# Moving the turned activation to the front of SBUF, and the down projection's stationary operand behind the branch sum

## The reference, cut to what matters

```python
def swiglu(x, w_in, w_out):
    gate, up = jnp.split(x @ w_in, 2, axis=-1)
    return (jax.nn.silu(gate) * up) @ w_out
...
    for layer in range(DEPTH):
        ff = swiglu(rmsnorm(h, g[0]), ffn_w_in[layer, 0], ffn_w_out[layer, 0])
        h = h + 0.5 * rmsnorm(ff, g[1])
        ...                                   # mixer: attention, gated linear attention or RWKV
        ff = swiglu(rmsnorm(h, g[4]), ffn_w_in[layer, 1], ffn_w_out[layer, 1])
        h = h + 0.5 * rmsnorm(ff, g[5])
```

## Time and profile before

| What | us |
|---|---|
| median of 3 runs | 3006.59 (3006.22 to 3006.69) |
| the profiled execution | 3007.35 |
| its span, first to last instruction | 3005.4 |
| PE busy | 2882.7 |
| DVE busy | 2102.8 |
| ACT busy | 1448.9 |
| GB/s from and to HBM, mean over the span | 156 |

### The profile page before, as it was taken

The page is one execution under the profiler, slowest core; times in us unless marked ns, Lnnn a source line. Parts: engine busy times, 40 slices in busy tenths (PEclk is TensorE's granted clock), DMA queues, the critical chain, the costliest instruction groups (busy, mean ns, idle before and its releaser), DMA issues.

```text
span 3005.4 us, 44680 instructions
## 1 busy us (share of the span) xinstructions
PE 2882.7 (96%) x17202; PEld 2491.9 (83%) x17202; DVE 2102.8 (70%) x3035; ACT 1448.9 (48%) x1865; POOL 84.4 (3%) x94
## 2 busy tenths in 40 slices
PE   8998999999999999999999999998999999989998
PEld 7887787888888888888988878876887889978887
DVE  6767677776767777767767777766777775565676
ACT  5445545445544444563444454455445444444443
POOL 0000000000000000100120000000000000000000
PEclk9999999999999999999999999999999999999999
DMA  8643564663456566431016656643656656533662
GB/s 241 207 115 127 173 196 142 210 191 114 133 179 196 157 189 207 121 121 50 1 53 186 196 153 198 185 126 120 189 182 175 189 159 183 183 116 129 200 195 84
DMA packets 614848, 471.24 MB, mean 157 GB/s; under 512 B 40545, under 2 KB 572385, under 8 KB 614708
## 3 DMA queue, kind: packets, MB, share of 16 engines
q1 hardware_dynamic: 614564, 469.31, 51.7%
q10 hardware_dynamic: 144, 0.00, 0.0%
HBM read 466.37 MB, written 1.84 MB: 156 GB/s over the span
## 4 chain that ended last, share of the span: by engine, by line
PE 84%; DVE 8%; ACT 5%; issue 2%; DMA 0%; SPq 0%; PEldq 0%; ACTq 0%; DVEq 0%; PEld 0%
PE pair_bank L413 26%; PE pair_bank L414 14%; PE pair_bank L589 11%; PE out_banks L433 7%; PE out_banks L435 7%; PE out_banks L434 7%; PE out_banks L589 2%; DVE low L337 2%; ACT high L333 2%; PE pair_bank L406 1%; PE pair_bank L2200 1%; PE pair_bank L2188 1%; DVE h L733 1%; PE pair_bank L2184 1%; DVE y L723 1%
## 5 line engine op out<-in xcount | busy, mean ns | idle before, releaser
L337 DVE TENSOR_TENSOR low<-raw,high 128x3072 fp32r<-128x3072 f32 (+2 forms) x328 | 934.7, 2850 | 603.7 <-ACT high L333 602.9
L413 PE MATMUL pair_bank<-x_parts,high 128*128 128x512 f32 x3360 | 1179.1, 393 | 4.4 <-issue 2.4
L414 PE MATMUL pair_bank<-x_parts,low 128*128 128x256 f32 x3520 | 961.9, 280 | 0.0
L333 ACT ACTIVATE high<-raw 128x3072 fp32r<-128x3072 f32 (+2 forms) x328 | 774.0, 2360 | 255.2 <-PE out_banks L435 154.0
L413 PEld LDWEIGHTS pair_bank<-x_parts,high 128*128 128x128 f32 x3360 | 629.6, 187 | 150.3 <-issue 7.8
L414 PEld LDWEIGHTS pair_bank<-x_parts,low 128*128 128x128 f32 x3520 | 655.1, 189 | 10.7 <-DVE low L337 1.1
L463 ACT ACTIVATE sq_scratch<-pair_bank 128x512 f32<-128x512 f32 x220 | 131.6, 598 | 559.1 <-PE pair_bank L414 559.1
L433 PE MATMUL out_banks<-high,hid_h 128*128 128x512 f32 x880 | 348.5, 396 | 9.5 <-DVE hid_l L505 9.5
L434 PE MATMUL out_banks<-low,hid_h 128*128 128x512 f32 x880 | 347.9, 395 | 0.0
L435 PE MATMUL out_banks<-high,hid_l 128*128 128x512 f32 x880 | 347.8, 395 | 0.0
L589 PE MATMUL pair_bank<-high,x_parts 128*128 128x256 f32 x1216 | 232.1, 289 | 4.6 <-DVE x_parts L786 1.6
(11 more groups left out here) (374 smaller groups left out, 3060.6 us busy)
## 6 DMA issues: line engine op xcount, KB each, us to landing
raw<-in_ffn_w_in_dram SPq DMA_DIRECT2D x352, 512.0 KB
raw<-in_ffn_w_out_dram SPq DMA_DIRECT2D x176, 512.0 KB
raw<-in_ffn_w_dram SPq DMA_DIRECT2D x132, 512.0 KB
raw<-in_w_in_dram SPq DMA_DIRECT2D x32, 1024.0 KB
raw<-in_gla_w_in_dram SPq DMA_DIRECT2D x12, 1024.0 KB
raw<-in_rwkv_w_rkv_dram SPq DMA_DIRECT2D x12, 1024.0 KB
raw<-in_swa_w_qkv_dram SPq DMA_DIRECT2D x10, 1024.0 KB
raw<-in_swa_w_o_dram SPq DMA_DIRECT2D x8, 1024.0 KB
```

The lines of the kernel that those rows point to most:

```text
L333: nc.scalar.activation(high[u % SPLIT][:, lo:w], raw[u % RAW][:, lo:w], ACT.Copy).then_inc(high_ready, count)
L337: nc.vector.tensor_tensor(low[u % SPLIT][:, lo:w], raw[u % RAW][:, lo:w], high[u % SPLIT][:, lo:w].bitcast(F32), ALU.subtract).then_inc(we ...
L413: nc.tensor.matmul(o, H[:, w], x_parts[:, k, :], start=(k == 0), stop=False)
L414: last = nc.tensor.matmul(o[:, 0:SEQ], L[:, w], xh[:, k, :], start=False, stop=(k == KB - 1))
```

## The change

The allocation of `x_parts` is moved in front of the `raw` slots, and that of the four `hid` buffers from behind `hidden` to behind `y`. Nothing else is changed. Each engine's instructions are the same in the same order; only the addresses in them differ.

```diff
+        x_parts = sb("x_parts", [P, KB, 2 * SEQ], F32R)
         raw = [sb(f"raw{i}", [P, SLOT]) for i in range(RAW)]
         high = [sb(f"high{i}", [P, SLOT], F32R) for i in range(SPLIT)]
         low = [sb(f"low{i}", [P, SLOT], F32R) for i in range(SPLIT)]
         h = sb("h", [P, NT, D])
         y = sb("y", [P, NT, D])
-        x_parts = sb("x_parts", [P, KB, 2 * SEQ], F32R)
         xh, xl = x_parts[:, :, 0:SEQ], x_parts[:, :, SEQ:2 * SEQ]
+        hid_h = [sb(f"hid_h{i}", [P, SEQ], F32R) for i in range(2)]
+        hid_l = [sb(f"hid_l{i}", [P, SEQ], F32R) for i in range(2)]
         gain = [sb(f"gain{i}", [P, D]) for i in range(2)]
         gain_columns = [sb(f"gain_columns{i}", [P, KB]) for i in range(2)]
         silu = sb("silu", [P, SEQ])
         hidden = sb("hidden", [P, SEQ])
-        hid_h = [sb(f"hid_h{i}", [P, SEQ], F32R) for i in range(2)]
-        hid_l = [sb(f"hid_l{i}", [P, SEQ], F32R) for i in range(2)]
```

## The result

| | before | after |
|---|---|---|
| median, us | 3006.05 (3002.12 to 3007.37, 20 runs) | 3011.36 (3008.58 to 3016.67, 20 runs) |
| profiled execution: time / span, us | 3007.35 / 3005.4 | 3010.25 / 3008.3 |
| one unit, us | 8.35 | 8.39 |
| one down projection, us | 2.80 | 2.75 |
| gate and up: one pair, ns | 346.7 | 353.3 |

The changed kernel is slower: the ratio is 1.0022, with a 95% interval of 1.0016 to 1.0028. The forecast was 2989 us; the result lies 2 us beyond the upper end of the range, and on the other side of the time before.

A forecast was written before the change was run, and what follows sets the result against it. The prediction took PE's stream of matmuls, 96% busy, as the bound: 3006.6 - 17.6 (`hid` buffers) + 0 (`x_parts` and the rest) = 2989.0 us. Its own range was 2986 to 2992 us (0.58), the wide one 2986 to 3009 (0.85).

The forecast's parts named there:

- What bounds the kernel: Whole kernel: a stream of matmuls on PE, 96% busy, so time is their number times their pitch.
- The cause of the down projection's slow pitch: Down projection: 6.7 ns extra per matmul, laid to the `hid` buffers' place, 64 bytes beyond a multiple of 128, or high.
- The term for it: Down projection, L433 to L435: the `hid` buffers' move saves 6.7 ns on each of 2640 matmuls, 17.6 us.
- half of it: Down projection: some six of 12 matmuls stay at 232 ns, 9 us won, 2997.6 us; chance 0.06.
- The pairs: Gate and up, L413 and L414: the pairs stay at 346.7 ns, no change in time.
- The prediction's own sign for this: Profile after, gate and up: pairs at other than 346.7 ns would mean the move of `x_parts` counts.
- The term for `x_parts`: Matmuls reading `x_parts`, 10,288 counted: the move to a low address gives nothing, bounds 69 us either way.
- The waits: L433's wait for `hid_l`, 9.5 us in all, grows by less than 1 us; up to 0.8 us given back.
- The readings: Pitches from trace starts: 37 output-projection matmuls at 226.7 ns; after stalls, 6 at 232 and ten down-projection ones at 233.
- The one that named a time near the result, 3011.5 us: Low `x_parts` costs 6.7 ns a matmul: 3058 us if all pay, 3011.5 if only L413 does; chance 0.10.

The follow-up runs named there:

- The best kernel here: Kernel before with all 512-column matmuls ahead of the 256s, `hid` moved behind `y` on a multiple of 128, `x_parts` 64 bytes off: 2976.57 us, ratio 0.9895.

## Why the prediction was wrong, point by point

- **What bounds the kernel: right.** No wait of the changed kernel has grown by more than 2.3 us, and all that moved is pitch.
- **The cause of the down projection's slow pitch: right.** It is the alignment of the stationary operand and not its height, as the two kernels with `gain_columns` moved show. The Trainium skill, "SBUF — State Buffer", section "Who interferes with whom", has PE wait on nobody. Whatever makes the step, these runs show that a matmul's pitch does depend on where its operand starts, 226.7 or 233.3 ns.
- **The term for it: mis-sized.** The prediction gave all 12 matmuls of a down projection the settled pitch, 2640 x 6.7 = 17.6 us. Measured are 10.9 us within the down projections. The first five stay slow, at 232 ns in the mean, even with no stall ahead. This was the rival "half of it", with its 9 us, to which I gave 0.06. The earlier trace rows had shown the slow start, and I had tied it to stalls.
- **The pairs: the step that failed.** "It can act only through a pitch that depends on where an operand lies", and the pairs' operands keep their alignment, so they were given 346.7 ns again. They went to 353.3: +14.6 us, more than the down projection gives. The pitch of alternating lengths is not a property of their operands alone. At the addresses of these two kernels it has two values, and moving `hid`, which the pairs don't read, moved 189 units from the one to the other. So the alignment of `hid` acts on the pairs through the down projection ahead of them. The prediction's own sign for this was wrong too: it said that pairs at other than 346.7 ns would convict the move of `x_parts`.
- **The term for `x_parts`: right.** Its count of 10,288 left out, among others, the 160 matmuls of L406 and the 192 of the output projection, which would have widened its bounds from 69 to 71 us. The term itself is zero, by the run with that half alone: 1.0003, interval 0.9994 to 1.0012. The output projection with `x_parts` stationary stays at 226.7 ns: fifteen distances in 845.39 - 841.99 = 3.40 us.

```profile
841.99 0.39 PE L589 MATMUL out_banks<-low,x_parts 128*128 128x512 f32 x1
...
845.39 0.39 PE L589 MATMUL out_banks<-low,x_parts 128*128 128x512 f32 x1
```

- **The waits: right.** L433's wait for `hid_l` grew from 9.5 to 10.0 us.
- **The readings.** Where the earlier trace rows say 37, 6 and 10 matmuls between, these are the distances, and one matmul fewer stands between. The pitches worked out from them are right.
- **The rivals.** The one that named a time near the result, 3011.5 us, had the low place of `x_parts` as its mechanism, and that mechanism is not there.

The sum with the measured sizes, as an estimate: in the median over the units gate and up went from 5.555 to 5.640 us and the down projection from 2.798 to 2.747 us. 189 units that changed their rhythm x 0.085 us - 220 down projections x 0.051 us = 16.1 - 11.2 = +4.9 us, against +5.3 us between the medians of the two kernels.

Could it have been seen? The trace of before held ten units in the slow rhythm, the one at 332.69 among them. I had read six pairs of one unit and taken their pitch for all. The time of a down projection could be argued from rows; that the pairs had a second pace could be read off them. Which one the change would select could not, as far as I see.

**What stays open.** Why the pairs have two rhythms, and what in a fully aligned down projection makes them start in the slow one, is not settled. With `x_parts` aligned the runs give only the rule: all of the down projection aligned, slow; any sort 64 bytes off, fast; 32 bytes off, by turns; a stall at the entry can turn it either way. With `x_parts` 64 bytes off the pairs took 353.3 ns behind a down projection that was off too, and no run has the pairs, `x_parts` off and `hid` aligned.

Nor is it settled which alignment counts. Every buffer that is called aligned here begins 128 bytes beyond a multiple of 512, so a multiple of 128 was never told apart from that. And in no run were the stationary and the moving operand of one fp32r matmul both off by 64, so it may be their difference that counts and not the place of each.

## What to carry to other kernels

Before a pitch is multiplied by a count, look at it in several units and behind several entries: a stream of alternating lengths can hold two rhythms, and a trace shows the second one in its exceptions. When an edit quickens one stream, ask what the next stream inherits, and price a short stream with its slow start, five matmuls here, and not with its settled pitch alone. Equal lengths in a row, with an aligned stationary operand, kept the gain: here order and alignment gave 14 us together, while the order alone gave nothing and the alignment alone cost 5 to 9.

## What the runs showed of the hardware

- An fp32r matmul of 512 columns with a weight load of its own has a pitch of 226.7 ns when its stationary operand starts on a multiple of 128 bytes, and of 233 to 234 ns when it starts 32 or 64 bytes beyond, low or high in SBUF (147,648 or 157,888). With the moving operand 64 bytes off and the stationary one aligned, 16 such matmuls took 3.68 us, 230 ns each.
- With 256 columns the sign is the opposite: 120.0 ns on the multiple and 113 to 118 with one operand 64 bytes off it, for the moving as for the stationary operand. The best kernel here rests on it, and I know no reason for it.
- In the changed kernel a stream of 512 columns behind the pairs starts with five slow distances, between 228 and 236 ns, without any stall. Where the pairs stop at another point of their rhythm it has one, of 236 ns (the kernel that enters with two matmuls). A stream that follows one of the same length and pitch has none: in the unit with the 512s first, the 16 behind a settled down projection take 226.7 ns from the first on.
- Pairs of 512 and 256 columns with aligned operands have two stable rhythms, 346.7 and 353.3 ns, at the same addresses and the same granted clock, and keep the one they settle in for the whole unit.
